# Local attention: the q projection by head pair, laid between the scores and the transposes

## The reference

```
qkv = h @ w_in + b_in                      # 16 query heads and 4 key heads of 64
q = rope(q, 16 of 64 dims);  k = rope(k, 16 of 64 dims)
s = einsum(q, keys of this 64-token chunk and of the one before) * 64**-0.5   # masked before the start
p = softmax(concat([s, sink]))[..., :-1]   # a learned sink per head
y = einsum(p, values of the same two chunks) @ w_o + b_o
```

## Time and profile before

| | us |
|---|---|
| median of 3 runs | 2156.65 (2154.78 to 2157.03) |
| the profiled execution | 2155.57 |
| its span | 2153.8 |
| PE busy in the span | 2087.7 |
| DVE busy | 1169.2 |
| ACT busy | 814.1 |

### The profile page before, as it was taken

One profiled execution on the slowest core, in us unless ns is written; L12 is line 12 of the kernel. 1 busy time (PEld: TensorE's weight loads), 2 busy tenths in 40 slices (PEclk: granted clock), 3 DMA queues, 4 the chain that ended last, 5 costly groups with the idle time before them and its releaser, 6 DMA issues.

```text
span 2153.8 us, 25099 instructions
## 1 busy us (share of the span) xinstructions
PE 2087.7 (97%) x9834; PEld 1715.6 (80%) x9834; DVE 1169.2 (54%) x1359; ACT 814.1 (38%) x1154; POOL 175.5 (8%) x192
## 2 busy tenths in 40 slices
PE   8999999999989999999996999999999999999997
PEld 6778888888867888888884788888887778888886
DVE  6766543434878644444657564444466655434344
ACT  6554322313466423223335342322335643232231
POOL 5001000000110100004200010000420001000000
PEclk9999999999999999999998999999999999999998
DMA  6012322233223332222230122223231123322321
GB/s 184 26 59 81 105 95 96 93 97 98 79 71 105 98 97 94 94 96 98 91 98 21 59 94 95 95 97 97 99 102 33 39 78 108 97 96 92 97 97 40
DMA packets 113168, 188.00 MB, mean 87 GB/s; under 512 B 14912, under 2 KB 26048, under 8 KB 113088
## 3 DMA queue, kind: packets, MB, share of 16 engines
q1 hardware_dynamic: 112752, 186.83, 27.0%
q10 hardware_dynamic: 336, 0.07, 0.0%
HBM read 184.78 MB, written 2.10 MB: 87 GB/s over the span
## 4 chain that ended last, share of the span: by engine, by line
PE 87%; DVE 7%; ACT 4%; issue 1%; DMA 0%; SPq 0%; DVEq 0%; ACTq 0%
PE psum L531 27%; PE psum L533 27%; PE psum L532 27%; ACT arena L2094 1%; PE psum L835 1%; DVE w_lo L1138 1%; PE psum L822 1%; DVE arena L1447 1%; PE psum L675 1%; DVE small L1433 1%; ACT w_hi L1887 0%; ACT arena L2329 0%; DMA x<-in_x 0%; DVE small L1764 0%; PE psum L1037 0%
## 5 line engine op out<-in xcount | busy, mean ns | idle before, releaser
L1138 DVE TENSOR_TENSOR w_lo<-w_raw,w_hi 128x1024 fp32r<-128x1024 f32 x345 | 427.8, 1245 | 826.8 <-ACT w_hi L1887 825.9
L1887 ACT ACTIVATE w_hi<-w_raw 128x1024 fp32r<-128x1024 f32 x345 | 364.3, 1060 | 996.7 <-PE psum L533 996.4
L531 PE MATMUL psum<-h_hi,w_hi 128*128 128x512 f32 x1384 | 546.8, 395 | 5.1 <-DVE w_lo L1138 5.1
L533 PE MATMUL psum<-h_hi,w_lo 128*128 128x512 f32 x1384 | 540.0, 390 | 0.0
L532 PE MATMUL psum<-h_lo,w_hi 128*128 128x512 f32 x1384 | 539.9, 390 | 0.0
L531 PE MATMUL psum<-u_hi,w_hi 128*128 128x512 f32 x1336 | 526.3, 394 | 8.5 <-ACT arena L2209 7.2
L533 PE MATMUL psum<-u_hi,w_lo 128*128 128x512 f32 x1336 | 521.8, 391 | 0.0
L532 PE MATMUL psum<-u_lo,w_hi 128*128 128x512 f32 x1336 | 521.7, 391 | 0.0
L531 PEld LDWEIGHTS psum<-h_hi,w_hi 128*128 128x128 f32 x1384 | 260.7, 188 | 62.5 <-DVE w_lo L1138 6.0
L532 PEld LDWEIGHTS psum<-h_lo,w_hi 128*128 128x128 f32 x1384 | 260.6, 188 | 56.6 <-issue 3.4
L533 PEld LDWEIGHTS psum<-h_hi,w_lo 128*128 128x128 f32 x1384 | 260.4, 188 | 54.6
(11 more groups left out here) (241 smaller groups left out, 1393.0 us busy)
## 6 DMA issues: line engine op xcount, KB each, us to landing
w_raw<-in_mlp_w SPq DMA_DIRECT2D x256, 512.0 KB, 3.7
w_raw<-in_mla_w_o SPq DMA_DIRECT2D x16, 512.0 KB, 3.5
w_raw<-in_lru_w_in SPq DMA_DIRECT2D x16, 512.0 KB, 4.0
w_raw<-in_swa_w_in SPq DMA_DIRECT2D x12, 512.0 KB, 3.7
w_raw<-in_mla_w_ukv SPq DMA_DIRECT2D x8, 512.0 KB, 4.3
w_raw<-in_lru_w_out SPq DMA_DIRECT2D x8, 512.0 KB, 3.5
w_raw<-in_swa_w_o SPq DMA_DIRECT2D x8, 512.0 KB, 3.5
w_raw<-in_mla_w_in SPq DMA_DIRECT2D x7, 512.0 KB, 3.8
```

Of the source, the lines that this page charges most:

```text
L531: nc.tensor.matmul(out, stat[0], mov[0], start=start, stop=False, skip_group_check=skip)
L533: return nc.tensor.matmul(out, stat[1], mov[0], start=False, stop=stop, skip_group_check=skip)
L1138: nc.vector.tensor_tensor(w_lo[:, to], w_raw[:, to], exact(w_hi[:, to]), ALU.subtract).then_inc(w_ready, 1)
L1887: nc.scalar.activation(w_hi[:, to], w_raw[:, to], ACT.Copy).then_inc(w_hi_done, 1)
```

## The change

The q projection is no longer two groups of four units but eight units, one per head pair, each with all 8 row blocks of the input for 128 output columns, into one bank. Its DMA moves rows of 512 B, where a unit before moved 2 KB. Pairs 0 to 2 are projected ahead of the first scores; then PE's order per pair i is scores(i), weighted(i-1), query(i+3), transposes(i), and the swap of pair i+2. From pair 5 on, blocks of the output projection's first group stand in the place of the query. Scores of all pairs and transposes now share area 2, the two banks of areas 0 and 1 hold a pair's q and its swapped rows, and DVE fills the masked corner anew for every pair. On DVE the multiplication of the probabilities comes in the same turn as the maximum, ahead of the next weight split. The keys' two copies are made by DVE (lower partitions) and ACT (upper ones).

```diff
     def swa():
         square("swa_in", 0, 1, 2)
-        square("swa_in", 0, 2)
+        u.extend(("swa_q", 0, i, PAIR) for i in range(KC))
         square("swa_o", 0, 2)
...
+                if kind == "swa_q":
+                    return A["swa_w_in"][u[1], :, u[2] * P:(u[2] + 1) * P].rearrange("(k p) n -> p k n", p=P)
...
+                query_area = [3, 1] + [i % 2 for i in range(2, KC)]
+                def query(i):
+                    next_unit_ready()
+                    a = query_area[i]
+                    claim(a)
+                    wh, wl = unit()
+                    for k in range(KC):
+                        at = slice(k * P, (k + 1) * P)
+                        mm = product(bank(a, 0), (wh[:, at], wl[:, at]), (HI[k], LO[k]), k == 0, k == KC - 1)
+                    mm.then_inc(unit_done, 1)
+                    used("query", i)
+                def swap_query(i):
+                    pe.wait_ge(biased, 2 + i + 1)
+                    swap_rows(bank(query_area[i], 1), 1, chunk(swa_m["q"], i)).then_inc(psum_done, 1)
+                    summed("swap", i)
...
                 def scores(i):
-                    claim(i % 2)
+                    if i == 0:
+                        pe.wait_ge(k_copied, 1)
+                    pe.wait_ge(mixed, 1 + i + 1)
+                    claim(2)
+                    pe.wait_ge(area_free[3], c.at("area3"))
...
-                for i in range(KC):
-                    if i in (0, 4):
-                        pe.wait_ge(mixed, 3 if i == 0 else 5)
-                    scores(i)
-                    if i == 0:
-                        swaps(2, 2)()
-                        swaps(3, 3)()
-                    if i >= 2:
-                        weighted(i - 2)
-                    if i >= 1:
-                        transposes(i - 1)
...
+                query(0)
+                swap_keys()
+                query(1)
+                swap_query(0)
+                query(2)
+                swap_query(1)
+                for i in range(5):
+                    scores(i)
+                    if i:
+                        weighted(i - 1)
+                    query(i + 3)
+                    transposes(i)
+                    swap_query(i + 2)
+                swap_query(KC - 1)
+                scores(5)
+                weighted(4)
+                out(0)
+                out(1)
+                transposes(5)
+                out(2, (0, 1))
...
+                scores(7)
+                weighted(6)
+                out(5)
+                out(6, (0, 1))
+                transposes(7)
+                out(6, (2, 3))
+                weighted(7)
+                out(7)
+                square_group((2, 3), UHI, ULO, anything)
...
# DVE
-                for i in range(KC + 1):
-                    if i < KC:
-                        largest(i)
-                    if i >= 1:
-                        normalised(i - 1)
...
-                    if i >= 2:
-                        head_lo(UHI[i - 2], ULO[i - 2])
-                    if i >= 1:
-                        sum_ready()
-                        c.add("area3")
-                        free(nc.vector.tensor_copy(m["pt"][:, 0:T], bank(2, 0)), 2)
+                for i in range(KC):
+                    if i <= 5:
+                        rotate_swapped(i + 1)
+                    if i == 5:
+                        rotate_swapped(7)
+                    largest(i)
+                    if i <= 5:
+                        rotate_rest(i + 1)
+                    if i == 5:
+                        rotate_rest(7)
                     if i >= 1:
+                        head_lo(UHI[i - 1], ULO[i - 1])
+                    normalised(i)
+                    if i + 3 < KC:
+                        rows_in(i + 3)
+                    split(1)
+                    done("transposes", i)
+                    nc.vector.tensor_copy(m["pt"][:, 0:T], bank(2, 0)).then_inc(area_free[2], 1)
...
# ACT
+                for i in range(KC):
                     if i >= 1:
+                        out_hi(i - 1)
+                    exponentials(i)
+                    split(1)
+                    if i + 3 < KC:
+                        query_bias(i + 3)
+                    done("transposes", i)
+                    nc.scalar.activation(m["pt"][:, T:2 * T], bank(2, 1), ACT.Copy).then_inc(area_free[3], 1)
```

More of the change, by code:

```diff
@@ L970, in swa, with summed, used @@
             def swa():
[L971 to L981, removed]
+                def summed(*name):
+                    c.add("psum_done")
+                    jobs["swa", *name] = psum_done, c.now("psum_done")
+                def used(*name):
+                    c.add("tensor_unit")
+                    jobs["swa", *name] = unit_done, c.now("tensor_unit")
                 hooks = {1: rotary_angles(1), 3: token_sums(2, ssq, 7)}
@@ L1071, in swa @@
[L1071 to L1081 removed]
+                    summed("weighted", i)
@@ new lines, in out @@
+                def out(k, ms=range(4)):
+                    if k % 2 == 0 and ms[0] == 0:
+                        next_unit_ready()
+                    if k == 0:
+                        jobs["swa", "before out"] = {name: c.now(name) for name in ("tensor_unit", "area0", "area1")}
+                        claim(0)
+                        claim(1)
+                    pe.wait_ge(area_free[4], outs_before + k + 1)
+                    wh, wl = unit()
+                    for m in ms:
+                        at = slice(k % 2 * T + m * P, k % 2 * T + (m + 1) * P)
+                        mm = product(bank(m // 2, m % 2), (wh[:, at], wl[:, at]), (UHI[k], ULO[k]), k == 0, k == KC - 1)
+                        if k == KC - 1 and m == 1:
+                            mm.then_inc(psum_done, 1)
+                            c.add("psum_done")
+                    if k % 2 == 1 and ms[-1] == 3:
+                        mm.then_inc(unit_done, 1)
+                        c.add("tensor_unit")
@@ new lines, in swa @@
+                out(0)
+                out(1)
+                transposes(5)
+                out(2, (0, 1))
+                scores(6)
+                weighted(5)
+                out(2, (2, 3))
+                out(3)
+                out(4, (0, 1))
+                transposes(6)
+                out(4, (2, 3))
+                scores(7)
[5 more added lines that the diff above has]
+                weighted(7)
@@ L1083, in _ @@
+                jobs["swa", "before out"] |= {name: c.now(name) for name in ("psum_done", "area2", "area3", "area4")}
+                out(7)
+                square_group((2, 3), UHI, ULO, anything)
             pe.wait_ge(ones_set, 1)
@@ L2341, in swa @@
-                head_hi(UHI[KC - 1])
-                split(4)
+                query_bias(0)
+                split(1)
+                act.wait_ge(k_rotated, 1)
+                for g in range(SW_G):
+                    ins = nc.scalar.activation(chunk(m["kd"], g)[64:P, :],
+                                               chunk(m["p"], g // 2)[64 * (g % 2):64 * (g % 2) + 64, :], ACT.Copy)
+                ins.then_inc(k_copied, 1)
+                query_bias(1)
+                split(1)
+                query_bias(2)
```

183 lines of the change are left out of this document (82 added, 101 removed).

## The result

The changed kernel takes 2133.38 us (median of 4 runs, 2131.77 to 2134.17) against 2156.84 for the kernel before (4 runs, 2154.78 to 2157.9): a ratio of 0.989, interval 0.9877 to 0.9904, or 23.5 us less. Forecast were 2132, range 2126 to 2142. A later comparison of the same two kernels gave 0.9893 (0.9876 to 0.991).

What follows compares the result with a forecast made beforehand. PE, busy for 97% of the span, loses 31.0 us in local attention to a softmax relay and slow clock. The block ends at 1218.4 instead of 1242.9, 24.5 us back: 2131.1, adjusted to 2132, range 2126 to 2142.

Steps and rivals of the forecast that it cites:

- What bounds the kernel: Local attention, 1139.1 to 1196.0: softmax relay with no matmul work beside it and a slow clock; 31.0 us lost.
- Up to the first scores: Local attention's start: first q product at 1090.16, three q units and swaps, first scores at 1109.95; DVE's key copies covered.
- The relay: One pair's softmax from the scores' start through DVE, ACT and DVE to the multiplication's end: 7.5 us.
- The steady pair: Pairs 0 to 4: PE's work is 9.5 us, but DVE's copy delays the next scores, so the period is 10.2.
- The waits: PE's remaining waits in local attention: 1.4 us in pair 0, 2.0 in the next three, 0.5 in pair 5, 2.7 at the end.
- S: The time at which PE starts a pair's scores; later events of that pair are counted from it.
- Transfers: Loads of q units in 512 B pieces: 7.6 us each, low bound 3.8, needed some 30 us later; cost zero.
- (A): Rival: DVE's copy comes earlier, PE hardly waits, the period is 9.5; about 4 us back, 2128; chance 0.14.
- (B): Rival: DVE becomes the bound, with 11.5 us per pair and long waits of scores for the copy; 2142; chance 0.16.
- (C): Rival: q units wait for their area until the relay's end, period 14.8; about 2155, no change; chance 0.04.
- (D): Rival: short idles drop PE's clock, a pair takes about 18 us; 2194 with all pairs, 2163 with four; chance 0.04.
- The total: Whole kernel: 24.5 us off the profiled 2155.57 gives 2131.1; with run median and handovers added, 2132.

Runs made afterwards that it cites:

- the version with the split moved: Changed kernel with the weight split moved: on ACT to the turn's start, on DVE ahead of the multiplication except in pair 5; 2130.74 us, ratio 0.9881.
- the first experiment: Changed kernel with only DVE's weight split put ahead of the multiplication of the probabilities in each pair's turn; 2156.87 us, ratio 1.0007 to the kernel before.
- with the fill: Changed kernel with DVE's split ahead of the multiplication, plus unread products (11 or 6 per pair) ahead of the transposes' wait; 2147.77 us, ratio 0.9954.

## Why the prediction was right

*What bounds the kernel.* Right in the main. From the second pair on the stall was a relay with no matmul work beside it; the new order brought back 22.9 of the 31.0 us inside the block (24.5 forecast), and filling the waits with useless work (the kernel before, filled) 3.2. But the longest wait, 9.0 of the 19.2 us, is not the relay alone, and the prediction didn't look into it. DVE in the kernel before, behind the first scores:

```profile
1142.59 1.23 DVE L1298 TENSOR_TENSOR arena<-psum,sin 128x1024 f32<-128x1024 f32 x1 [0.44 <-PE psum L675]
...
1149.89 1.22 DVE L1138 TENSOR_TENSOR w_lo<-w_raw,w_hi 128x1024 fp32r<-128x1024 f32 x1
1151.03 1.22 DVE L1764 TENSOR_REDUCE small<-psum 128x8 f32<-128x1024 f32 x1
...
1153.00 1.22 DVE L1779 TENSOR_TENSOR arena<-arena,small 128x1024 f32<-128x1024 f32 x1
```

Six rotary operations (1142.59 to 1149.85), a weight split and the second pair's maximum stand in DVE's queue ahead of the first pair's multiplication, so its transposes begin 15.0 us behind its scores, where the relay takes 7.8. The changed kernel deals the rotations out, one pair's to a turn (two in pair 5) and under the exponentials, and so takes away this stall too. How much of the 22.9 us comes from that and how much from the q units beside the relay was not tried apart; 15.0 - 7.8 = 7.2 us is an estimate of the most that it can be.

*Up to the first scores.* From the first q product it took 19.81 us, forecast 19.79. The four copies of the keys took 0.42 us each, below the 0.69 that I took and inside the bounds.

*The relay.* Forecast 7.5, measured 7.84 in pair 0 (1107.92 to 1115.76) and 7.83 in pair 7. The term that was short by 0.24 is the exponentials, and the other 0.1 is in the handovers: I had taken 2.75 us, up to the start of the last row sum's read, as if that overlapped what follows. It does so for the next instruction of its own engine, which starts at 2.85 (1162.73 in the earlier trace rows). DVE waits for the read's end, so the whole 2.99 count. This is also what makes pair 0's turn 10.21 instead of 9.9.

*The steady pair.* The form was right: PE to the unit's end, then scaling, split and copy on DVE, 2.58 us to the next scores (2.6 forecast). The unit's end comes at 7.83 behind the scores instead of 7.6, and the periods are 10.42 instead of 10.2. This is the term that was mis-sized: a q unit is 5.71, not 5.45. I took 5.45 from a unit that came behind transposes (1196.09 in the earlier trace rows; its first product took 0.23 on the chain). Behind the weighted values the first product takes 0.43 (1130.74 in the chain above), and the other 0.05 is spread over the rest of the unit. I booked 0.5 us for all handovers together; it is 0.25 per unit. Over pairs 0 to 4 the sum is 52.03 against 50.9 (from 1107.92 to 1159.95), and the rest of the block 58.0 against 57.55. Altogether the stretch from the first scores is 110.04 against 108.45.

*The waits.* Forecast 1.4 us in pair 0, 2.0 in the next three, 0.5 in pair 5, and 1.3 and 1.4 at the end. Measured 1.46 (1.04 and 0.42), 1.9, none, 1.32 and 1.42. Pair 5 has none because its unit on PE ends at S + 7.8 instead of 7.6, while DVE's work between maximum and multiplication is 3.25 us instead of 3.4, so that its transposes could start at S + 7.93 instead of 8.1.

*Transfers.* They cost nothing, as forecast. The five q units issued from 1060 to 1160 us landed after 4.0 us (median), where the prediction had 7.6, twice the time of a load of half the size; no engine waited for them.

*The rivals.* (A) was wrong for this kernel, and the version with the split moved shows what it lacked. (B) has no sign: no period is over 10.6. (C) has none: no q unit waits for an area. (D) did not come; the first experiment shows how near it was. The changed kernel's waits of 0.63 us in turns of 10.4, and of 1.04, 1.32 and 1.42 us once each, left the clock at 1.00; the first experiment's waits of 2.07 us in turns of 13.4 brought it to 0.88. The prediction's grounds against (D) were weaker than its price for it. The stretch of the earlier trace rows that it leaned on has one such wait, not one in every turn, and that it had taken a wait of 9.0 us or an engine busy for half of the time no longer holds: in the first experiment PE was busy for 33.88 of 40.10 us when the clock was 0.88. That (D) stayed away was in part luck. I had priced it at about 18 us a pair with everything slow; where it came, mostly the transposes and what stood directly behind them ran slowly, some 1.6 us a turn, and then the clock was back. The Trainium skill (TensorE: Matmul & The Clock Gate, section "A second HAM failure mode: psum-queue depth-cycling") says that frequent short idles between groups of matmuls can make the clock swing; the first experiment's trace agrees for its waits of 2.07 us, and the changed kernel's shows none of it for its shorter ones.

*The total.* 23.5 us measured, 24.7 forecast (2156.65 - 2132). Inside the block 1.6 us less came back than the sum said. In the profiled executions 0.9 us of it was made up outside, by drift that has nothing to do with the change (2131.77 against the 2131.1 of the sum), so that the time is nearer than the working was; that is luck.

## What to carry to other kernels

When an engine waits inside a relay, first ask whether later work of its own can be cut so that a piece of it fits the wait; then walk the other engines' queues for what stands between the relay's links, since one instruction in front of a link, itself waiting for a third engine, gave all of the 23.5 us back. Where a unit of work moves between other kinds of matmuls, count its handovers per unit. An operation that covers another must be read to its end when the next one is on another engine. And where one wait is far longer than those that repeat, look for its own cause.

## What the runs showed of the hardware

- TensorE's clock was 0.88 over turns of 13.4 us with a wait of 2.07 us in each. Waits of 0.6 to 0.9 us in turns of 11.84 us (with the fill), and of 0.4 to 1.4 us in the changed kernel, left it at 1.00. The length of one wait didn't decide it: behind a single wait of 3.13 us the transposes still took 1.09 us.
- Products that nobody reads, issued where TensorE would wait, kept the clock at 1.00 (from 0.88, and from 0.59 where it had waited over 5 us a turn) and gave back 9 to 11 and 12 us. Put behind a semaphore that comes late, they cost 12 to 13 us instead.
- Behind a group of 64-wide matmuls, the first 512-column product was followed by the next after 0.33 us, and the last product of a unit by transposes after 0.37, where it was 0.23 within the unit.
- The read of a row sum on ACT overlapped ACT's next instruction (start to start 0.09 us for an instruction of 0.24), but DVE, which needs the sums, started only behind its end: eight exponentials were 2.85 us for ACT's next instruction and 2.99 for DVE.
- A copy of 64 partitions by 512 columns between on-chip buffers took 0.42 us on DVE, an addition of that shape 0.69.
